# Retention in three pairs of heads with their norms moved into the recurrences, and the four GLA heads scored in one step

## What is computed

```python
# retention, per head: decay = gamma^(i-j) for i >= j
o_t = sum_{m<=t} gamma^(t-m) (q_t . k_m) v_m
# HGRN and GLA, per head: a gate for every key dimension
S_t = diag(a_t) S_{t-1} + k_t v_t^T ;  o_t = S_t^T q_t
# then for each head
o = o * rsqrt(mean(o*o) + eps) * gain * silu(gate)
merged @ w_out_2
```

## Time and profile before

| | |
|---|---|
| median of three runs | 1473.83 us |
| the profiled execution, its own time | 1473.85 us |
| its span, first to last instruction | 1471.7 us |
| PE busy | 1341.0 us (91%) |
| DVE busy | 647.7 us (44%) |
| ACT, POOL busy | 388.1 us, 265.1 us |
| mean granted TensorE clock | 0.939 of full |

### The profile page before, as it was taken

One profiled execution on the slowest core, in us unless ns is written; L12 is line 12 of the kernel. 1 busy time (PEld: TensorE's weight loads), 2 busy tenths in 40 slices (PEclk: granted clock), 3 DMA queues, 4 the chain that ended last, 5 costly groups with the idle time before them and its releaser, 6 DMA issues.

```text
span 1471.7 us, 17619 instructions
## 1 busy us (share of the span) xinstructions
PE 1341.0 (91%) x7291; PEld 1038.8 (71%) x7291; DVE 647.7 (44%) x795; ACT 388.1 (26%) x488; POOL 265.1 (18%) x238
## 2 busy tenths in 40 slices
PE   5999999999899999999997999989988869998861
PEld 4888888777788888888866888758877745544430
DVE  3323533256455473655645232336552436443324
ACT  5223444342432231312243322241121300000001
POOL 0410000002021020301100000822332013332212
PEclk9999999999999999999988999977689879999996
DMA  5232322543236253462402232212004969999964
GB/s 206 86 114 99 102 86 87 178 151 127 103 116 245 97 205 138 171 228 114 178 27 90 86 106 94 86 45 86 2 1 147 411 259 415 416 417 418 417 246 171
DMA packets 44260, 249.13 MB, mean 169 GB/s; under 512 B 10101, under 2 KB 10757, under 8 KB 17441
## 3 DMA queue, kind: packets, MB, share of 16 engines
q1 hardware_dynamic: 36514, 228.73, 40.9%
q0 software_dynamic: 7104, 17.35, 3.1%
q10 hardware_dynamic: 576, 2.10, 0.4%
HBM read 240.26 MB, written 17.06 MB: 175 GB/s over the span
## 4 chain that ended last, share of the span: by engine, by line
PE 78%; DMA 8%; DVE 4%; ACT 3%; issue 2%; SPq 2%; POOL 1%; POOLq 0%; ACTq 0%; DVEq 0%
PE ps L329 20%; PE ps L330 20%; PE ps L331 20%; DMA experts<-in_w_exp 6%; PE ps L2088 4%; PE ps L1949 3%; PE ps L2106 2%; SPq L537 2%; PE ps L1686 1%; PE ps L283 1%; DMA h<-experts 1%; PE ps L1876 1%; PE ps L2076 1%; PE ps L1704 1%; ACT arena L261 1%
## 5 line engine op out<-in xcount | busy, mean ns | idle before, releaser
L314 DVE TENSOR_TENSOR w_low<-raw,w_high 128x2048 fp32r<-128x2048 f32 x81 | 214.6, 2650 | 263.7 <-ACT w_high L310 263.7
L329 PE MATMUL ps<-u_high,w_high 128*128 128x512 f32 (+1 forms) x712 | 279.4, 392 | 0.0
L331 PE MATMUL ps<-u_high,w_low 128*128 128x512 f32 (+1 forms) x712 | 277.3, 389 | 0.0
L330 PE MATMUL ps<-u_low,w_high 128*128 128x512 f32 (+1 forms) x712 | 277.1, 389 | 0.0
L310 ACT ACTIVATE w_high<-raw 128x2048 fp32r<-128x2048 f32 x81 | 154.6, 1909 | 181.9 <-PE ps L331 153.0
L329 PEld LDWEIGHTS ps<-u_high,w_high 128*128 128x128 f32 (+1 forms) x712 | 132.9, 187 | 30.7 <-issue 1.7
L331 PEld LDWEIGHTS ps<-u_high,w_low 128*128 128x128 f32 (+1 forms) x712 | 132.9, 187 | 28.8
L330 PEld LDWEIGHTS ps<-u_low,w_high 128*128 128x128 f32 (+1 forms) x712 | 132.9, 187 | 28.2 <-issue 0.2
L329 PE MATMUL ps<-w_high,v_high 128*128 128x512 f32 x320 | 126.4, 395 | 5.1 <-POOL v_low L1538 5.1
L330 PE MATMUL ps<-w_low,v_high 128*128 128x512 f32 x320 | 125.7, 393 | 0.0
L331 PE MATMUL ps<-w_high,v_low 128*128 128x512 f32 x320 | 125.5, 392 | 0.0
(11 more groups left out here) (368 smaller groups left out, 1818.2 us busy)
## 6 DMA issues: line engine op xcount, KB each, us to landing
raw<-in_w SPq DMA_DIRECT2D x82, 1024.0 KB
experts<-in_w_exp SPq DMA_DIRECT2D x69, 1024.0 KB
arena<-in_w_exp SPq DMA_DIRECT2D x30, 1024.0 KB
arena<-in_w_ada SPq DMA_DIRECT2D x24, 1024.0 KB
gates<-arena POOLq DMA_DIRECT2D x16, 256.0 KB, 3.0
arena<-gates POOLq DMA_DIRECT2D x2, 2048.0 KB, 9.3
arena<-y SPq DMA_DIRECT2D x8, 512.0 KB, 7.5
x<-in_x SPq DMA_DIRECT2D x1, 2048.0 KB, 7.5
```

The source lines that it names most:

```text
L314: dve.tensor_tensor(WL[:, 1 - s, :], RAW[:, 1 - s, :], WH[:, 1 - s, :].bitcast(F32), ALU.subtract).then_inc(lo_ready, 1)
L329: pe.matmul(out, a[0], b[0], start=start, stop=False)
L330: pe.matmul(out, a[0], b[1], start=False, stop=False)
L331: return pe.matmul(out, a[1], b[0], start=False, stop=stop)
```

## The change

Retention runs in three pairs. PE scores both heads of a pair side by side (one from rows 0 to 63, one from rows 64 to 127, in different banks), DVE multiplies both with one instruction per block shape, and PE sums both. The decay tables have two double buffers and their DMAs are issued right after the 16-column projection (`ga_mm`); the mask is loaded behind the first four of them. DVE's first multiplication no longer waits for the gate chain nor stands behind the split of unit K0+1; that split's ACT half moves behind the norm of tile 2, its DVE half to step 44. Of the retention tiles' norms only that of tile 0 stays ahead of the recurrences; the value sum of pair 2 and the norms of tiles 1 and 2 are placed between steps 3 and 21.

In the recurrences the steps of pair 4 fall away: at a step of pair 3 PE issues 16 matmuls for the four GLA heads from row groups 0, 32, 64 and 96 into banks 0 to 3, and DVE copies all four with one masked copy twice as wide. Buffers move to make room (`NEAR`, `FAR`, `RET`, `GT`).

```diff
-            sp.wait_ge(unit_done, K0)
-            sp.dma_start(MASK, t["masks"].bitcast(U32)).then_inc(mask_in, 16)
-            for h in range(6):
-                if h == 0:
-                    sp.wait_ge(rope_d, 6)
-                else:
-                    sp.wait_ge(ret_a, h)
-                sp.dma_start(DT, t["decay"][h, :, :]).then_inc(d_in, 16)
+            sp.wait_ge(ga_mm, 1)
+            for j in range(3):
+                if j == 2:
+                    sp.dma_start(MASK, t["masks"].bitcast(U32)).then_inc(mask_in, 16)
+                    sp.wait_ge(ret_a, 4)
+                for hh in range(2):
+                    sp.dma_start(DT[:, j % 2, hh, :], t["decay"][2 * j + hh, :, :]).then_inc(d_in[j % 2], 16)
...
-            split_hi(act, 0, K0 // 2, 0)
             for i in range(3):
                 head_norm(i)
+            split_hi(act, 0, K0 // 2, 0)
...
-            dve.wait_ge(ga_f, 4)
-            dve.scalar_tensor_tensor(TRG[:, 2, :], TRG[:, 0, :], 0.0, TRG[:, 1, :], ALU.min, ALU.subtract).then_inc(ga_f, 1)
-
-            split_lo(dve, 0, K0 // 2, 0)
-
...
+            def retention(j):
+                near = RET[j % 2][:, 0:1024].rearrange("p (h c s) -> p h c s", h=2, c=4)
+                far = RET[j % 2][:, 1024:2560].rearrange("p (h s) -> p h s", h=2)
+                decay = DT[:, j % 2, :, :]
+                dve.wait_ge(d_in[j % 2], 32 * (j // 2 + 1))
+                dve.wait_ge(ret_s, 3 * j + 1)
+                dve.tensor_tensor(near, PS[:, 0:2, :].rearrange("p h (c s) -> p h c s", c=4), decay[:, :, 0:P].unsqueeze(2).broadcast_to([P, 2, 4, P]), ALU.mult).then_inc(ret_a, 1)
+                dve.wait_ge(ret_s, 3 * j + 2)
+                dve.tensor_tensor(far[:, :, 0:384], PS[:, 2:4, 0:384], decay[:, :, P:512], ALU.mult).then_inc(ret_a, 1)
+                dve.tensor_tensor(far[:, :, 640:768], PS[:, 2:4, 384:512], decay[:, :, P:256], ALU.mult).then_inc(ret_a, 1)
+                dve.wait_ge(ret_s, 3 * j + 3)
+                dve.tensor_tensor(far[:, :, 384:640], PS[:, 4:6, 0:256], decay[:, :, P:384], ALU.mult).then_inc(ret_a, 1)
+            retention(0)
+            dve.wait_ge(unit_done, K0)
+            dve.wait_ge(hf_d, 9)
+            retention(1)
+            dve.wait_ge(ga_f, 4)
+            dve.scalar_tensor_tensor(GT[:, 2, :], GT[:, 0, :], 0.0, GT[:, 1, :], ALU.min, ALU.subtract).then_inc(ga_f, 1)
+            head_root(0)
+            dve.wait_ge(ret_o, 1)
+            retention(2)
+            head_gate(0)
             dve.wait_ge(mask_in, 16)
             dve.wait_ge(tot_d, 14)
...
                 p, lev = ORDER[s]
+                i = 16 if p == 3 else 8
+                dst, src = NEAR_GLA if p == 3 else diag_scores(p), PS[:, 0:4, :] if p == 3 else score_banks(s)
+                src = src.rearrange("p b n -> p (b n)").rearrange("p (i s) -> p i s", i=i)
                 if lev < 0:
-                    if s < 3:
-                        dve.wait_ge(ab_zero, BUF[p] + 1)
...
-                    else:
-                        dve.wait_ge(pass_o, 1 + BUF[p])
-                    dst, src = diag_scores(p).rearrange("p (i s) -> p i s", i=8), score_banks(s).rearrange("p h n -> p (h n)").rearrange("p (i s) -> p i s", i=8)
-                    own = MASK[:, 0, :].unsqueeze(1).broadcast_to([P, 8, P])
+                    dve.wait_ge(ab_zero, 3) if s < 3 else dve.wait_ge(pass_o, 1 + BUF[p])
+                    dst = dst.rearrange("p (i s) -> p i s", i=i)
+                    own = MASK[:, 0, :].unsqueeze(1).broadcast_to([P, i, P])
                 else:
                     m = 1 << lev
                     dve.wait_ge(lvl_a, copied(STEP[p, lev - 1]))
-                    dst = diag_scores(p).rearrange("p (i n two m) -> p i n two m", i=8, two=2, m=m)[:, :, :, 1, :]
-                    src = score_banks(s).rearrange("p h n -> p (h n)").rearrange("p (i s) -> p i s", i=8)[:, :, 0:64].rearrange("p i (n m) -> p i n m", m=m)
-                    own = halves(MASK[:, lev + 1, :], lev)[:, :, 1, :].unsqueeze(1).broadcast_to([P, 8, 64 // m, m])
+                    dst = dst.rearrange("p (i n two m) -> p i n two m", i=i, two=2, m=m)[:, :, :, 1, :]
+                    src = src[:, :, 0:64].rearrange("p i (n m) -> p i n m", m=m)
+                    own = halves(MASK[:, lev + 1, :], lev)[:, :, 1, :].unsqueeze(1).broadcast_to([P, i, 64 // m, m])
                 dve.copy_predicated(dst, own, src).then_inc(lvl_a, 1)
...
-                dve.wait_ge(lvl_s, s + 1)
-                if p != 3 and lev < 8:
+                dve.wait_ge(lvl_s, s + (2 if p == 3 else 1))
+                if p != 4 and lev < 8:
                     decay_queries(p, lev)
-                if lev <= 6:
+                if p != 4 and lev <= 6:
                     near_scores(s)
-                if s in (4, 32, 39, 46):
-                    head_root({4: 2, 32: 3, 39: 4, 46: 5}[s])
-                elif s in (8, 35, 42, 49):
-                    head_gate({8: 2, 35: 3, 42: 4, 49: 5}[s])
+                if s in (5, 15, 32, 39, 46):
+                    head_root({5: 1, 15: 2, 32: 3, 39: 4, 46: 5}[s])
+                elif s in (8, 18, 35, 42, 49):
+                    head_gate({8: 1, 18: 2, 35: 3, 42: 4, 49: 5}[s])
+                elif s == 44:
+                    split_lo(dve, 0, K0 // 2, 0)
...
                         for hh in range(2):
                             out = PS[64 * hh:64 * hh + 64, 6, :]
-                            val = V2[:, cs, 64 * (6 + 2 * p + hh):64 * (6 + 2 * p + hh) + 64]
+                            val = V2[:, cs, P * tile + 64 * hh:P * tile + 64 * hh + 64]
                             pe.matmul(out[:, P * cs + P:S], val, far[:, hh, at[cs]:at[cs] + P * (3 - cs)], start=False, stop=False, skip_group_check=True)
-                last.then_inc(pass_o, 1)
+                last.then_inc(signal, 1)
+
+            def retention_scores(j):
+                if j:
+                    pe.wait_ge(ret_a, 4 * j - 3)
+                for c in range(NC):
+                    for hh in range(2):
+                        q_, k_ = [RQK[64 * hh:64 * hh + 64, x + j, :] for x in (0, 3)]
+                        last = pe.matmul(PS[:, hh, P * c:P * c + P], k_[:, P * c:P * c + P], q_[:, P * c:P * c + P], start=True, stop=True)
+                last.then_inc(ret_s, 1)
+                if j:
+                    pe.wait_ge(ret_a, 4 * j - 1)
+                for hh in range(2):
+                    q_, k_ = [RQK[64 * hh:64 * hh + 64, x + j, :] for x in (0, 3)]
+                    pe.matmul(PS[:, 2 + hh, 0:384], k_[:, 0:P], q_[:, P:S], start=True, stop=True)
+                for hh in range(2):
+                    q_, k_ = [RQK[64 * hh:64 * hh + 64, x + j, :] for x in (0, 3)]
+                    last = pe.matmul(PS[:, 2 + hh, 384:512], k_[:, 2 * P:3 * P], q_[:, 3 * P:S], start=True, stop=True)
+                last.then_inc(ret_s, 1)
+                if j:
+                    pe.wait_ge(ret_a, 4 * j)
+                for hh in range(2):
+                    q_, k_ = [RQK[64 * hh:64 * hh + 64, x + j, :] for x in (0, 3)]
+                    last = pe.matmul(PS[:, 4 + hh, 0:256], k_[:, P:2 * P], q_[:, 2 * P:S], start=True, stop=True)
+                last.then_inc(ret_s, 1)
+
+            def retention_sum(j):
...
+            retention_scores(0)
+            pe.wait_ge(z2_out, 10)
+            pe.matmul(PS[:, 7, :], WH[0:16, 1, P:2 * P].bitcast(F32), GA, start=True, stop=False)
+            pe.matmul(PS[:, 7, :], WL[0:16, 1, P:2 * P].bitcast(F32), GA, start=False, stop=True).then_inc(unit_done, 1)
+            retention_scores(1)
+            retention_sum(0)
+            retention_scores(2)
+            pe.wait_ge(ga_f, 1)
+            mean_square(0)
+            retention_sum(1)
+            spread_root(0)
...
-                out, rows = score_banks(s), [rows_of(p, hh) for hh in range(2)]
+                if p == 3:
+                    out, rows = PS[:, 0:4, :], [rows_of(3 + hh // 2, hh % 2) for hh in range(4)]
+                else:
+                    out, rows = score_banks(s), [rows_of(p, hh) for hh in range(2)]
...
-                if s == 7:
+                if ORDER[s][0] != 4:
+                    scores(s)
+                if s == 3:
+                    mean_square(1)
+                elif s == 5:
+                    retention_sum(2)
+                elif s == 8:
+                    spread_root(1)
+                elif s == 14:
+                    mean_square(2)
+                elif s == 17:
                     spread_root(2)
             weigh_pair(3, 3)
```

154 lines of the change are left out of this document (49 added, 105 removed).

## The result

The changed kernel takes 1453.74 us (median of 4 runs, 1450.56 to 1456.3) against 1474.91 us (4 runs, 1473.52 to 1478.9). The ratio is 0.9846, 95% interval [0.9827, 0.9866]. The forecast was 1451 us, range 1441 to 1461. The profiled execution took 1453.94 us (span 1451.7, mean granted clock 0.940); DVE is busy for 647.7 us as before, with 775 instructions instead of 795, and PE for 1321.1 us instead of 1341.0.

The account below looks back on a forecast made before the run. Bound: the expert stage waits for the last head tile, and the 161.1 us before it are retention's wait chain and PE at 1.2 GHz. -26.9 + 2.5 + 0 + 0.6 + 1.8 = -22.0 gives 1452, stated as 1451, range 1441 to 1461.

Parts of the forecast that it names:

- Retention, -26.9: From the 16-column projection's end to the first level: 20.6 us instead of 47.5, by pairs, early tables and moved norms.
- DVE without a wait for a decay table: Sign in retention: DVE would no longer wait for decay tables, where each head had waited 2.82 us.
- Levels -1 to 1, +2.5: First recurrences: PE work moved in from retention and wider DVE copies lengthen these levels from 16.0 to 18.5 us.
- Levels 2 to 6, 0: First recurrences: the merged step's saving is used up by tile 2's norm and waits, so 23.9 us as before.
- a level is then 3.5 on PE: Levels 2 to 6: merged GLA step 1.6 us plus HGRN step 1.9, where a level took 4.8.
- the four-row-group step pays for the norms: Levels 2 to 6: the merged GLA step's saving covers the norm work moved in, and no more.
- Levels 7 and 8, +0.6: Last two levels of the first recurrences: 6.2 us instead of 5.6, as ACT still makes one copy a pair.
- the rest, +1.8: Second recurrence: the weight unit's split behind step 44 delays a query decay; 1.8 of its 2.3 to 2.5 us show.
- The expert stage, 0: From 1122.5 us on, the stage keeps its length and starts earlier by whatever the work before it saves.
- More clock: Rival, chance 0.22: half of levels 0 to 6 run at 2.4 GHz; -26 to -30 us, 1444 to 1448.
- take turns: Rival, chance 0.15: the four row groups do not overlap, a merged step costs 2.5 to 2.9 us; 1456 to 1461.
- stay at 1.2 GHz behind the levels: Rival, chance 0.03: the 68.1 us stretch loses its clock, 36 us more, giving 1488, slower than before.

Follow-up runs that it names:

- e11: Changed kernel with DVE multiplying the third pair ahead of the first norm's reciprocal, gate product left in place: 1450.1 us, ratio 0.9821.
- e5: Changed kernel with the norms of tiles 1 and 2 and the third pair's value sum put back ahead of the recurrences: 1459.6 us, ratio 0.9895.
- e6: Changed kernel with the second pair's decay table asked for only when the first pair is multiplied: 1452.1 us, ratio 0.9843.
- e2: Changed kernel with the merged GLA step undone, two steps of two heads with a narrow copy each: 1451.9 us, ratio 0.9835.
- e1: Kernel before with only the merge of GLA's four heads into one step and one masked copy: 1472.8 us, ratio 0.9993.
- e10: e5 with GLA's query decay moved from DVE to POOL as well: 1458.6 us (one run).
- e3: Changed kernel with the merged GLA step issuing heads 0 and 1, then 2 and 3, two row groups at a time: 1458.0 us, ratio 0.9886.
- e7: Changed kernel with GLA's query decay at each level below 8 moved from DVE to POOL: 1449.7 us, ratio 0.9834.
- e8: Changed kernel with the gate product ahead of the first pair's scores and the third pair ahead of the first reciprocal: 1449.0 us, ratio 0.9812.
- e9: Changed kernel with the edits of e8, e7 and e4, and the gate's sum taken inside the second pair: 1448.0 us, ratio 0.9834.
- e12: Changed kernel with the edits of e8, e7 and e4 together, the gate's sum left behind the second pair: 1448.0 us, ratio 0.9804.
- e4: Changed kernel with the low half of the weight unit split on DVE at step 26 instead of 44: 1451.4 us, ratio 0.9830.

## Why the prediction was right, and where it was not

The median is 2.7 us above the forecast and inside its range. The mechanism was right where most of the gain is, in retention and its norms. The sum is closer than its terms: by the windows -29.2, +2.5, -0.2, +1.1 and +3.1, together -22.7 for a forecast of -22.0, with 2.3 us more won in retention than forecast and 1.8 more lost in levels 7 and 8 and the rest. That these cancel is luck.

**Retention, -26.9: right in kind, 2.0 too small.** From the projection to the first level step are 18.5 us where I had 20.6, so -28.9. POOL's products took 6.2 us (973.31 to 979.50) and not the 8.1 of the earlier trace rows, and PE's value sum of the first pair ended at 972.7, not 973.8. My start of 964.6 for the tables was nearly met (964.99), but the claim "DVE without a wait for a decay table" failed for the first one (3.67 us): I had worked out that DVE starts when it lands and still called it no wait. I did not see the third pair queued behind the reciprocal (4.35 us of waiting, though only 0.2 us to win, e11). Nor did I ask which half of the change makes the gain. e5 parts it: of the 28.9 us, 11.7 are pairs (47.4 to 35.7), with the first multiplication freed from gate and split and the tables asked for ahead (about 2 us, e6), and 17.2 are the norms moved, of which 8.0 come back in the levels. Of the 22.3 us up to the expert stage the norms are 8.1 (e5) and the merge 0.9 (e2) or 3.3 (e1), depending on what stands beside it. That leaves 10.9 to 13.3 for the pairs, which no run has alone.

**Levels -1 to 1, +2.5: right, with luck in the number** (18.5 forecast and measured). The wide copies took 2.44 to 2.45 us for the forecast 2.6, and 1.23 to 1.34 from level 2 on for the forecast 1.34. The moved PE work was cheaper than I had it, since the clock was high for 8.3 of the 18.5 us (0.72 in the windows), where I had reckoned with 1.2 GHz throughout. What made up for it are PE's waits for the GLA copies: it was busy for 15.53 of the 18.5 us and idle for 2.17 before 984.15 and 0.84 before 998.25. With the clock of e6 and e11 the same instructions would have taken 1.4 us less.

**Levels 2 to 6, 0: right by two errors that cancel.** The merged step was taken at 1.6 and "a level is then 3.5 on PE". Measured 3.81 (e1, e10): the 0.34 us of hand-over between 32-row and 64-row steps is in the old 2.9 and was left out of the new 1.6, and the old steps overlapped already. The rows for it stood in the forecast (weight loads 83 ns apart against 111) and I used them for the row groups alone. Against it worked the clock, 0.56 and not 0.50. "3.4 to 3.6 us from one to the next" was 3.69 between 1001.18 and 1004.87, and 3.8 in e1, e5 and e10. The sentence that the four-row-group step pays for the norms holds in a weak form: 4.6 us of norms in levels 2 to 6 (e5) against 3.3 (e1), and in the whole time the merge cannot be seen.

**Levels 7 and 8, +0.6, and the rest, +1.8: 1.1 and 3.1 measured.** The split alone, where it shows, is 2.6 (e2). In the changed kernel the lower clock covers it, 10.2 us at 1.2 GHz around steps 44 to 48 where there were 3.4. The term was mis-sized and its cause was only one of two.

**The expert stage, 0: 2.7 given back in the profiled run.** The windows of its last 5% of matmuls, before and changed:

```profile
1416.30:1441.90 25.60, 14.96 (x94) 7.48 (x90) 4.99 (x13) 0.56 (x2) 5.15 (x9) 0.87 0.38 144
```
```profile
1394.10:1422.40 28.30, 17.41 (x93) 8.18 (x90) 4.78 (x13) 0.56 (x2) 5.10 (x9) 0.76 0.34 129
```

Where they begin, both are level within 0.4 us from the start of the stage. Then PE is busy 2.45 us longer at a clock of 0.76 in the place of 0.87. Of the profiles, before, e1, e3, e5, e10 and e11 have 25.3 to 25.9 there and changed, e2, e6, e7, e8, e9 and e12 have 28.3 to 28.5, with e4 between. What decides it I did not find; it goes with no part of the change (e3 and e11 hold all of retention's). e3 and e11 gain another 2.3 us in the first quarter of the stage, which gives their 346 to 347 us; the cause of that is open too.

**The rivals.** More clock: in part. Levels -1 to 1 had 0.72 and levels 2 to 6 0.56, so the full clock for 11 of their 42 us and not for half. The row groups do not take turns (e3: that would be +4.5 in the levels, just under my +5 to +9). The clock did not stay at 1.2 GHz behind the levels, though some of that rival came true: 0.86 for 0.89. The rule that would speak for more clock (an engine kept busy gets the full clock; the Trainium skill, TensorE: Matmul & The Clock Gate, Why this matters for your kernels) is again not what the trace shows: 0.50 in e5 with PE busy for 98% of 19.3 us.

## What to carry to other kernels

A serial chain over several engines (copy, square, sum, root, spread, gate) costs its latency where it stands alone and less where it stands among other work: here 17.2 us against 8.0 for two tiles. Before two steps are merged for parallel row groups, look at the weight loads in the trace: if the steps overlap already, the merge saves only what is left, and a wide copy replaces two that overlapped with PE. Two stalls of like size in the same place can be paid once, so that removing one shows nothing (e4); remove both before calling one of them free. And before a stage's gain is put down to an edit, look at the granted clock and at PE's busy time there, and at a run without the edit: 1.4 us that looked like those of e8 and e11 stood in e6 as well.

## What I had not expected of the hardware

Two PE steps that follow each other in different row groups run interleaved without being written so (14 weight loads start in 0.64 us, where 10 start in 0.92 in one step alone), while 0.34 us pass between a step of 32-row and one of 64-row products at 1.2 GHz, in either order, and 0.20 at 2.4 GHz (changed kernel, before 995.27). Between two 64-row steps there is no such gap (32 matmuls in one row from 1081.40 in the earlier trace rows). The masked copy of 1024 elements takes 2.44 us at levels 0 and 1 and 1.23 to 1.34 from level 2 on. The same instructions took 32.2 or 34.9 us with the granted clock at 0.94 or 0.89, and the tail of the expert stage 25.6 or 28.3 at 0.87 or 0.76: together more than what most edits of this study moved.
